# Keys and values of one projection by Strassen's identity over pairs of row tiles, with the query weights loaded last

## The reference, cut to what matters

```
z = h @ w_in                       # h: 1088 rows x 1024
nq, nkv, ng, fq, fk, fv, ff, ga, gb = jnp.split(z, idx, axis=-1)
# nkv 768 wide, ng 24, ff 8; fk and fv ("forget" keys and values) 512 each; nq, fq 512 each (queries)
```

## Time and profile before

| | us |
|---|---|
| median of 3 runs | 2430.34 (2428.55 to 2432.49) |
| the profiled execution | 2436.32 |
| its span | 2434.5 |
| PE busy | 2370.6 (97% of the span) |
| DVE busy | 1238.5 (51%) |
| POOL busy | 831.1 (34%) |
| ACT busy | 547.9 (23%) |
| mean granted TensorE clock | 0.996 of full speed |

### The profile page before, as it was taken

The page is one execution under the profiler, slowest core; times in us unless marked ns, Lnnn a source line. Parts: engine busy times, 40 slices in busy tenths (PEclk is TensorE's granted clock), DMA queues, the critical chain, the costliest instruction groups (busy, mean ns, idle before and its releaser), DMA issues. The chain is left out here.

```text
span 2434.5 us, 30908 instructions
## 1 busy us (share of the span) xinstructions
PE 2370.6 (97%) x10983; PEld 1532.2 (63%) x10983; DVE 1238.5 (51%) x3115; ACT 547.9 (23%) x1328; POOL 831.1 (34%) x874
## 2 busy tenths in 40 slices
PE   8999999999998999899999999999999999999999
PEld 4544665555556677688886458888888874443343
DVE  4876716776773444522322794433334324229775
ACT  0001016666663333111111221111011110001131
POOL 0000004554454000475753453334333237203540
PEclk9999999999999999999999999999999999999999
DMA  5423730021028886532225301111111115434101
GB/s 185 106 82 86 272 112 20 1 87 53 1 63 222 242 230 188 201 93 78 87 71 158 83 31 53 35 36 53 35 52 37 35 56 206 162 143 147 71 26 48
DMA packets 185955, 240.28 MB, mean 99 GB/s; under 512 B 53435, under 2 KB 128833, under 8 KB 184265
## 3 DMA queue, kind: packets, MB, share of 16 engines
q1 hardware_dynamic: 181018, 218.99, 28.8%
q0 software_dynamic: 3616, 9.73, 1.2%
q10 hardware_dynamic: 1168, 9.58, 1.2%
HBM read 216.18 MB, written 37.99 MB: 104 GB/s over the span
## 5 line engine op out<-in xcount | busy, mean ns | idle before, releaser
L2218 PE MATMUL ps<-xT,arena 128*128 128x272 f32 x1920 | 472.6, 392 | 0.0
L2218 PEld LDWEIGHTS ps<-xT,arena 128*128 128x128 f32 x1920 | 363.9, 190 | 75.3 <-issue 0.8
L2218 PE MATMUL ps<-queries,arena 128*128 128x272 f32 x1312 | 333.3, 394 | 3.9 <-DVE arena L1375 2.2
L2218 PEld LDWEIGHTS ps<-queries,arena 128*128 128x128 f32 x1312 | 250.1, 191 | 56.7 <-DVE arena L1375 2.6
L236 PE MATMUL ps<-arena,xT 128*128 128x512 f32 (+1 forms) x512 | 198.2, 549 | 2.2 <-DMA arena<-in_w_in 1.3
L1008 POOL TENSOR_SCALAR arena<-arena,gates 128x55 f32<-128x55 f32 (+15 forms) x192 | 123.5, 653 | 176.7 <-DVE arena L907 176.4
L943 ACT ACTIVATE arena<-arena 128x640 f32<-128x640 f32 (+15 forms) x256 | 164.7, 643 | 69.4 <-DVE arena L899 49.4
L236 PEld LDWEIGHTS ps<-arena,xT 128*128 128x128 f32 x512 | 97.7, 191 | 102.3 <-issue 93.0
L2218 PE MATMUL ps<-arena 128*128 128x272 f32 x576 | 149.6, 396 | 0.3 <-DVE arena L1366 0.3
L798 PE MATMUL ps<-ident,arena 128*128 128x128 f32 (+4 forms) x880 | 137.9, 284 | 11.1 <-POOL arena L1008 5.2
L786 PE MATMUL ps<-arena,queries 64*128 64x512 f32 (+11 forms) x704 | 129.3, 467 | 14.4 <-DVE arena L899 11.7
(11 more groups left out here) (345 smaller groups left out, 3272.6 us busy)
## 6 DMA issues: line engine op xcount, KB each, us to landing
arena<-in_cache_fox_kv SPq DMA_DIRECT2D x72, 256.0 KB, 4.5
arena<-in_w_ffn_down SPq DMA_DIRECT2D x68, 256.0 KB, 3.4
arena<-in_w_in SPq DMA_DIRECT2D x16, 1024.0 KB, 5.1
xT<-in_w_ffn_down SPq DMA_DIRECT2D x64, 256.0 KB, 3.6
xT<-in_cache_fox_kv SPq DMA_DIRECT2D x56, 256.0 KB, 6.0
arena<-in_cache_nsa_kv SPq DMA_DIRECT2D x64, 192.0 KB, 7.8
arena<-in_w_ffn_up SPq DMA_DIRECT2D x11, 1024.0 KB, 5.2
arena<-in_w_ffn_gate SPq DMA_DIRECT2D x11, 1024.0 KB
```

The lines of the kernel that those rows point to most:

```text
L2218: mm = pe.matmul(ps[:, first + BANK_OF[z], 0:PIECE], weight[:, j, :], moving[:, j, :], start=(j == 0 and z in (1, 6, 5, 7)), stop=(j == kk ...
```

## The change

The forget keys and values of the eight prompt tiles are computed by a Strassen (Winograd) form. Tiles p and p+4 make a pair; the 2x2 blocks are (tile p, tile p+4) x (first, second half of the 1024 terms) for the rows, and (first, second half of the terms) x (`fk`, `fv`) for the weights. Seven products of four matmuls take the place of eight (`forget_pair`, product order 1, 6, 7, 5, 2, 4, 3). POOL makes the four sums of the weights once (128x2048 each) and four sums of the rows for each pair (128x512 each). They lie in `keep.queries`. Products 2, 4 and 3 accumulate in PSUM onto 1, 7 and 5; ACT copies product 1 and the result `fk` of tile p, DVE adds the rest (five additions of 128x512 for each pair, the values straight into `keep.fv`).

The tile order is now 0, 4, 1, 5, 8, pair 0, 2, pair 1, 6, pair 2, 3, pair 3, 7, where a tile means its `kv4` and `win` pieces. Two key blocks of a tile are turned in one set of 16 transposes of 32x64 (`turn_keys`) instead of 32 of 32x32. The load of the third tile's rows goes ahead of the forget weights. The forget pages are issued eight per tile. The query weights of all four groups are loaded in one go, once pair 3's last addition is done (`r_step` 20), because the sums lie in their place until then. Semaphores of the first block are given back at the start of the prompt's attention.

```
+ROW_SEQ = (("K", 0), ("K", 4), ("K", 1), ("K", 5), ("S", 8), ("F", 0), ("K", 2), ("F", 1), ("K", 6), ("F", 2), ("K", 3), ("F", 3), ("K", 7))
+ROW_PRODUCTS = (1, 6, 7, 5, 2, 4, 3)
...
+    t1, t2, t4 = (flat[:, 2048 * j:2048 * (j + 1)].rearrange("p (k n) -> p k n", k=4) for j in range(3))
+    s1, s2, s3, s4 = (flat[:, 6144 + 512 * j:6656 + 512 * j].rearrange("p (k n) -> p k n", k=4) for j in range(4))
...
 rows_sync, after the weights of kv4 and win:
+        sp.wait_ge(x_turned, 2)
+        load(2)
         (weights of fk, weights of fv)
+        for kind, i in ROW_SEQ:
+            if kind == "F":
+                a, b = i, i + 4
+                sp.wait_ge(r_step, 5 * i + 3)
+                values_out(b)
+                sp.wait_ge(corner_staged, i + 1)
+                sp.dma_start(io["o_fox_kv"][cols(a), 0:FW], fk_a).then_inc(fk_stored, 16)
+                sp.wait_ge(r_step, 5 * i + 4)
+                sp.dma_start(io["o_fox_kv"][cols(b), 0:FW], fk_b).then_inc(fk_stored, 16)
+                sp.wait_ge(r_step, 5 * i + 5)
+                values_out(a)
+                continue
+            y = place(i)
+            if 1 <= y and y + 2 < NT:
+                sp.wait_ge(x_saved, y)
+                load(y + 2)
...
+            if y >= 1:
+                forget_pages(pages[8 * (y - 1):8 * y])
+            rows_out(y)
...
+            if i == 3:
+                sp.wait_ge(r_step, 20)
+                for g in range(NG):
+                    query_weights(sp, keep, io, g)
...
 rows_tensor:
+        def forget_pair(p):
+            a11, a12, a21, a22 = corners(p)
+            f = {1: (a11, b11), 6: (s2, t2), 7: (s3, b12), 5: (s1, t1), 2: (a12, b21), 4: (a22, t4), 3: (s4, b22)}
...
+                for j in range(4):
+                    mm = pe.matmul(ps[:, ROW_BANK[z], :], weight[:, j, :], moving[:, j, :], start=(j == 0 and z in (1, 6, 5, 7)), stop=(j == 3),
...
 rows_gpsimd, between the copies of tiles:
+        nc.gpsimd.tensor_tensor(t1, b12, b11, ALU.subtract).then_inc(t_summed, 1)
+        nc.gpsimd.tensor_tensor(t2, b22, t1, ALU.subtract).then_inc(t_summed, 1)
+        copies(3)
+        pair_sums(0)
+        pool.wait_ge(sample_ready, 2)
+        nc.gpsimd.tensor_tensor(b12, b22, b12, ALU.subtract).then_inc(t_summed, 1)
+        nc.gpsimd.tensor_tensor(t4, b21, t2, ALU.subtract).then_inc(t_summed, 1)
...
 prompt_attention, ahead of its block:
+        k.retire(over)
```

More of the change, by code:

```diff
@@ L155, in turn_blocks, with turn_keys @@
     return ins
+ROW_ORDER = (0, 4, 1, 5, 8, 2, 6, 3, 7)
+ROW_SEQ = (("K", 0), ("K", 4), ("K", 1), ("K", 5), ("S", 8), ("F", 0), ("K", 2), ("F", 1), ("K", 6), ("F", 2), ("K", 3), ("F", 3), ("K", 7))
+ROW_PRODUCTS = (1, 6, 7, 5, 2, 4, 3)
+ROW_BANK = {1: 4, 2: 4, 6: 5, 5: 6, 3: 6, 7: 7, 4: 7}
+def turn_keys(nc, out, rows):
+    m = rows.shape[0]
+    for q in range(4):
+        for z in range(m // 32):
+            ins = nc.vector.transpose(out[q * 32:(q + 1) * 32, :, z * 32:(z + 1) * 32], rows[z * 32:(z + 1) * 32, :, q * 32:(q + 1) * 32])
+    return ins
 def project_rows(k, keep, io):
@@ L180, in project_rows, with place, cols, corners @@
     tiles = [(i * P, min(P, R - i * P)) for i in range(NT)]
+    def place(i):
+        return ROW_ORDER.index(i)
+    def cols(i):
+        return slice(tiles[i][0], tiles[i][0] + tiles[i][1])
+    def corners(p):
+        return tuple(keep.xT[:, h:h + 4, cols(i)] for i in (p, p + 4) for h in (0, 4))
+    def products_until(p, z):
+        return len(ROW_PRODUCTS) * p + ROW_PRODUCTS.index(z) + 1
     def rows_sync(sp):
-        def load(i):
-            t0, m = tiles[i]
-            sp.dma_start(x_rows[0:m, i % 2, :], io["x_all"][t0:t0 + m, :]).then_inc(x_in[i % 2], 16)
+        def load(y):
+            t0, m = tiles[ROW_ORDER[y]]
+            sp.dma_start(x_rows[0:m, y % 2, :], io["x_all"][t0:t0 + m, :]).then_inc(x_in[y % 2], 16)
         def forget_pages(some):
@@ L226, in rows_tensor @@
-    def rows_tensor(pe):
[L227 to L246, removed]
-                    if c == KD - 1:
-                        mm.then_inc((kv4_ready, win_ready, fk_ready, fv_ready)[n], 1)
+        sp.dma_start(w_rows[:, :, 512:792], w_in[:, :, C_KV + 512:C_KV + 792]).then_inc(weights_in[1], 16)
@@ L256, in rows_tensor @@
             mm.then_inc(x_turned, 1)
[L257 to L260, removed]
-            else:
[L262 to L275, removed]
+        for kind, i in ROW_SEQ:
+            if kind == "K":
+                keys_and_gates(i)
+            elif kind == "S":
+                sample_rows(i)
+            else:
+                forget_pair(i)
     def rows_scalar(act):
@@ L315, in rows_gpsimd @@
-    def rows_gpsimd(pool):
+        embedding(1)
+        embedding(2)
+        keys(0)
+        embedding(3)
+        keys(1)
+        embedding(4)
+        keys(2)
+        embedding(5)
+        sample(8)
+        keys(3)
+        middle(0)
+        keys(4)
+        sides(0)
+        forget_keys(0)
+        embedding(6)
+        middle(1)
+        keys(5)
+        sides(1)
+        forget_keys(1)
+        embedding(7)
+        middle(2)
+        embedding(8)
+        sides(2)
+        keys(6)
@@ L679, in prompt_attention @@
     nc, ps, bank = k.nc, k.ps, k.bank
+    over = [s for s in k.live if s not in (keep.wf_in[NG - 1], *keep.slc_in)]
     with ExitStack() as local:
```

284 lines of the change are left out of this document (207 added, 77 removed).

## The result

| | us |
|---|---|
| before, median of 5 runs beside the changed kernel's | 2430.75 (2428.55 to 2433.47) |
| after, median of 5 runs | 2443.93 (2438.95 to 2446.13) |
| ratio after / before | 1.0045, 95% interval 1.0034 to 1.0056 |
| the profiled execution after (before) | 2443.93 (2436.32) |
| its span (before) | 2442.1 (2434.5) |

The changed kernel is slower: by 0.45% (10.9 us) by the ratio, by 13.2 us between the two medians. It lies above the range that was given (2415 to 2433).

A forecast was written before the change was run, and what follows sets the result against it. PE, 97% busy, was taken to bound the kernel. Terms -13.7 - 1.3 + 7.1 + 4.0 = -3.9 us gave 2432.4 against the profiled 2436.32, or 2426.4 for the median; range 2415 to 2433.

The forecast's parts named there:

- What PE saves: Row projection: 16 fewer matmuls save 13.7 us and the 1.27 us weight wait goes; rows end at 206.1.
- No wait inside the stage: Row projection: POOL, DVE and SP keep up with PE in the written order, each at cost 0.
- the thin margin of POOL at pair 0: Row projection: POOL's third weight sum ends near 71.6, product 7 wants it at 73.8; 2.2 us, cost 0.
- rival D: Row projection: POOL or DVE makes PE wait in each pair, 2 us a pair; +4 or -7 us; chance 0.05.
- SP is held by the query weights, the table is issued at 224.8: After pair 3: 12 query-weight DMAs hold SP until 211.9; `c_onehot` is issued at 224.8, against 223.65 before.
- Rival B: Query weights don't hold SP or drain much faster; table within 3 us, clock stays up; -15 to -9 us; chance 0.25.
- rival C: SP's queue holds longer, 6.6 us per group; table lands at 234, PE idles 14.7 us; +4, 2434; chance 0.1.
- PE waits 7.1 us: After `nsa(0)`: PE is done at 220.9 and waits for the table, landing at 228.0; +7.1 us, bounds 0 and 15.
- The clock, 4.0 us: Table and `fox(0)`: after PE's idle stretch the clock falls before the table's five matmuls; +4.0 us, bounds 0 and 5.
- The rows loaded back from HBM and the large bias writes have over 10 us each. Cost 0.: After the table: reloaded rows and bias writes each have over 10 us of slack, so cost 0.
- SP is 1 us later than before, PE 4 us earlier: After the stage: the shifts of SP and PE, with later PE work moving along if nobody else is late.

The follow-up runs named there:

- The last run above: Changed kernel with the query weights of groups 1 to 3 loaded after `c_onehot`, group 0's left in place: 2443.73 us, ratio 1.0047.
- `fox(0)` first: Changed kernel with PE doing `fox(0)`, the second half of group 0's queries, before it waits for the bias table: 2428.69 us, ratio 0.9995.
- the page loads alone: Changed kernel with SP's last eight small page loads moved ahead of its wait for `r_step` 20: 2433.23 us, ratio 1.0001.
- ACT's order without the wait: Changed kernel, `fox(0)` before the table wait, ACT copying the turned gates before the bias writes without waiting for the reloads: 2433.61 us, ratio 1.0002.
- the fastest version: Changed kernel, `fox(0)` before the table wait; ACT copies the turned gates, waits for the reloads, then issues the bias writes: 2419.06 us, ratio 0.9949.
- the kernel before with ACT's order and wait: Kernel before, with ACT copying the turned gates, then waiting for the reloads, then issuing the bias writes: 2432.04 us, ratio 0.9998.

## Why the prediction was wrong

- **What PE saves** (-15.0): right. 15.4 measured; the rows end at 205.63 for 206.1.
- **No wait inside the stage** (cost 0 on POOL, DVE, SP): right. PE has no gap up to 205.63, the thin margin of POOL at pair 0 held, rival D is out.
- **SP is held by the query weights, the table is issued at 224.8**: 224.74. The hold was near: SP was free at 210.6, 1.3 us before the forecast 211.9. That the issue came out to 0.1 us is luck, since what stands behind the hold took 14.1 us instead of 12.9. Rival B (the queue takes them) is out, rival C (the queue holds longer) too. The last run above confirms the mechanism: with three of these DMAs instead of twelve the table leaves 11.6 us earlier.
- **PE waits 7.1 us**: 8.25. `c_onehot` landed 0.7 us later than taken and PE was 0.5 us earlier.
- **The clock, 4.0 us**: the mechanism was right, the size was too small. The granted clock after, from 228.00 on:

```profile
228.00:233.60 5.60, 3.26 (x4) 0.36 (x4) 2.56 (x10) 3.94 (x7) 0.00 (x0) 0.50 0.86 188
...
238.40:242.70 4.30, 4.30 (x8) 2.46 (x8) 0.00 (x0) 1.67 (x3) 0.00 (x0) 0.50 0.83 124
242.70:255.00 12.30, 12.30 (x41) 7.59 (x40) 0.00 (x0) 0.00 (x0) 0.00 (x0) 0.97 0.92 284
```

  It is at the lower level from the first table matmul to 242.7. The term is 6.4: 5.3 on the table and 1.1 on `fox(0)`. Of the 5.3, 1.67 is a wait for ACT that I hadn't foreseen (its activations stand ahead of the copies), and the other 3.7 meet the forecast 3.6; `fox(0)` was forecast at 0.4. With the measured sizes the stage comes to -0.8 instead of -3.9. Up to here the forecast would have missed by 3 us and stayed inside its range.
- **"The rows loaded back from HBM and the large bias writes have over 10 us each. Cost 0."** This is the step that failed. It cost 8.3 us in the profiled execution, and taking it out gave 7.8 in the runs (6.6 by the ratios). The sentence looked at each of the two transfers against its own user, and the reloads do have 26 us there in the kernel before. It never set one against the other. The text just ahead of it had what was needed, "SP is 1 us later than before, PE 4 us earlier": ACT's writes are released by PE's table and SP's reloads by SP's queue, they lay 2.6 us apart, and the change moved them towards each other by 2.9 (0.9 and 2.0), after which the reloads' own issue, 6.70 us before, took 7.88. No row of the two issues was read.

None of the rivals held this case. The two on the slower side, C and D, came to 2434 by a longer hold and by waits inside the pairs; the traces show neither.

The Trainium skill ("DMA: Bandwidth & Descriptors", queues, rings and completion order) says that each DMA engine takes turns, packet by packet, between the queues that have work for it. No trace here shows the turns themselves. The page after has a queue with 1168 packets for 9.58 MB, 8.2 KB each, which by its bytes is ACT's (eight writes of 1160 KB), and a reload moves 128 KB in 256-byte runs, as the source of the kernel has it:

```profile
q10 hardware_dynamic: 1168, 9.58, 1.2%
```

An estimate from that, with each run taken as a packet of its own: a reload's 512 runs are 32 for each of 16 engines; at the 315 GB/s of the window 246 to 256 us an 8.2 KB packet holds one engine for 0.4 us, so a reload of which every run has to let one packet pass takes 13 us, and what SP queued beside it takes turns of its own. The landings of 22 to 37 us lie above it. In the changed kernel the last reload lands at 280.2, when every write must have landed already (the last is issued at 247.0, and none takes more than 32.8), which looks more like standing behind the writes than like taking turns with them. With `fox(0)` first it landed at 265.7, when the slowest write, at 34.2 us from an issue at 243.3 or later, was still under way, so there it did not stand behind all of them. How the writes delay the reloads stays open.

What is shown is that they do. With writes issued before the last reload had landed, the slowest reload took 22.0 to 36.9 us in five traces (after, the kernel before with late reloads, `fox(0)` first, the page loads alone, ACT's order without the wait). With the writes behind the reloads it took 4.8 to 5.2 us in seven (before, and the six with ACT's wait), and 7.5 in the one in which it follows the first write by more than 35 us (the last run above).

**What stays open.** The traces of after and before differ by 7.6 us and the medians of their five runs by 13.2. Before's profiled execution lay 5.6 above that median, after's on its own. From the start of the attention to the end of the span the profiled executions of these kernels, whose program is nearly the same there, took between 2088.6 us (2415.1 - 326.47, the fastest version) and 2096.7 (2436.3 - 339.60, the kernel before with ACT's order and wait), with 2094.4 both after (2442.1 - 347.67) and before (2434.5 - 340.15). So up to 8 us of a comparison of single traces can't be laid to what the edit does ahead of the attention. What makes them differ was not tried. Nor was moving the query weights to where no large write follows; every run here keeps them behind `r_step` 20.

## What to carry to other kernels

When one engine gets faster, list the DMAs that it releases on every queue and set their new issue times against the issue times on the other queues, not only against their users; two that cleared each other by 2 or 3 us are a term of the sum. A spread between runs that grows from 6 us to 15, 18 or 25, as in three versions here, can be the mark of such a near miss. Its absence clears nobody: the changed kernel has the full collision and a spread of 7. Where a transfer of short runs must not meet a large one, a wait on the large one's engine fixes the order for little, if nothing that others need stands behind that wait.

## What the runs showed of the hardware

- Large writes on one DMA queue go with a stall of another engine's issue, not only of its data. SP's eight reload issues took 6.70 us before, 21.94 and 35.67 where ACT's writes ran beside the last or all of them, and a single DMA took 29.10 us to issue.
- It goes both ways, by which comes first. In the four traces in which SP's 4608 KB store was issued 1.3 to 2.0 us ahead of the eight bias writes (before, and three versions with ACT's wait), ACT took 11.2 to 12.2 us to issue these; in the other nine, with the store behind the writes or more than 10 us ahead, 5.3 to 6.7. No run changed the store alone.
- The margin is a few us. A last reload issued 2.6 us ahead of the first write landed within 5.0 us; issued 0.3 or 0.4 us behind it, it took 30.9 and 22.0.
- What SP has issued just before decides how long it is held: 12 DMAs of 1024 runs in a row held it for 14.8 us (195.8 to 210.6), and where only the first three of them stood there, it was through with them in 2.0 (196.88 to 198.84).
